# Row sums in the projection banks, another order of the projection groups, two moved products in a streaming encoder layer on eight cores

## The reference, cut to what matters

```python
q, k, v, logf, g_fox, b_gate, u, g_conv, mq, g_mem = _project(x, w_in, fox_bf)   # u = c_gate * h_in
# A) forgetting attention, 12 heads x 128, causal
s = einsum(q, k) * 128**-0.5 + cum[query] - cum[key]        # cum = cumsum(logf)
o_fox = einsum(softmax(where(causal, s, -1e30)), v)
# B) y = b_gate * conv3(u), causal, depthwise, 1536 channels; a sample's u starts with two cached columns
# C) memory cross-attention, 4 heads x 256 into 256 tokens
gates = sigmoid(x @ w_merge + b_merge)                      # g1, g2, g3
m = g1*((o_fox*silu(g_fox)) @ w_fox_out) + g2*((o_conv*silu(g_conv)) @ w_conv_out) + g3*((o_mem*silu(g_mem)) @ w_mem_out)
y = layernorm(2**0.25 * x + m @ w_o)
```

## Time and profile before

| | us |
|---|---|
| median of 3 runs | 3396.12 (3395.94 to 3399.55) |
| the profiled execution, its own time | 3396.83 |
| span of its slowest core, core 4, which the rows show | 3395.1 |
| spans of the eight cores | 3386.3 to 3395.1 |
| TensorE busy | 3283.1 |
| VectorE, ScalarE, GpSimd busy | 1227.6, 906.3, 847.0 |
| mean granted TensorE clock, core 4 | 0.991 |

### The profile page before, as it was taken

One profiled execution on the slowest core, in us unless ns is written; L12 is line 12 of the kernel. 1 busy time (PEld: TensorE's weight loads), 2 busy tenths in 40 slices (PEclk: granted clock), 3 DMA queues, 4 the chain that ended last, 5 costly groups with the idle time before them and its releaser, 6 DMA issues.

```text
span 3395.1 us, 54170 instructions; the slowest of 8 cores (3386.3 to 3395.1 us)
## 1 busy us (share of the span) xinstructions
PE 3283.1 (97%) x18645; PEld 1638.8 (48%) x18998; DVE 1227.6 (36%) x2041; ACT 906.3 (27%) x1572; POOL 847.0 (25%) x1046
## 2 busy tenths in 40 slices
PE   6999999999998999999999999999999999999998
PEld 3555555555544444444444444445544444444443
DVE  0477777777775222222211111111102331111465
ACT  0355555555553111111111111111113331111111
POOL 2233333333333222222200000222221113222233
PEclk8999999999999999999999999999999999999999
DMA  9554534343432121212134433866661115665543
GB/s 156 101 98 81 88 75 83 73 86 75 82 61 39 30 44 32 41 35 37 36 83 108 109 89 90 177 144 144 150 150 30 25 26 130 138 145 144 199 160 124
DMA packets 156405, 315.76 MB, mean 93 GB/s; under 512 B 32784, under 2 KB 60048, under 8 KB 151708
## 3 DMA queue, kind: packets, MB, share of 16 engines
q0 software_dynamic: 43840, 134.54, 24.1%
q1 hardware_dynamic: 112296, 177.73, 17.8%
HBM read 351.42 MB, written 95.32 MB: 132 GB/s over the span
## 4 chain that ended last, share of the span: by engine, by line
PE 92%; DMA 3%; issue 2%; DVE 1%; ACT 1%; POOL 0%; DVEq 0%; ACTq 0%; POOLq 0%; SPq 0%
PE bank L146 92%; DMA xT<-xTp 1%; DMA m_scr<-mt 1%; DVE st L181 0%; DMA fk_p<-k 0%; DVE acc L173 0%; ACT k L168 0%; DMA wcb<-wcM 0%; ACT rl L163 0%; DVE rr L181 0%; PE bank L149 0%; ACT sc L163 0%; ACT ge L163 0%; DVE pt L173 0%; POOL wv L155 0%
## 5 line engine op out<-in xcount | busy, mean ns | idle before, releaser
L146 PE MATMUL bank<-xT,wcb 128*128 128x512 bf16 (+1 forms) x3757 | 715.2, 342 | 9.8 <-DMA wcb<-wcM 4.7
L146 PE MATMUL bank<-xT,cwb 128*128 128x512 bf16 (+1 forms) x3766 | 693.9, 342 | 3.9 <-issue 0.2
L146 PE MATMUL bank<-xT,wkqg 128*128 128x512 bf16 (+1 forms) x2812 | 595.7, 344 | 18.3 <-DMA wkqg<-wkqg 5.9
L173 DVE TENSOR_TENSOR mt<-bank,gt 128x512 f32<-128x512 f32 (+1 forms) x240 | 143.6, 598 | 1033.8 <-PE bank L146 940.0
L146 PEld LDWEIGHTS bank<-xT,wcb 128*128 128x128 bf16 x3840 | 326.8, 98 | 366.9 <-issue 8.1
L146 PEld LDWEIGHTS bank<-xT,cwb 128*128 128x128 bf16 x3840 | 324.0, 98 | 362.4 <-issue 4.3
L163 ACT ACTIVATE pt<-st,ncc 128x512 bf16<-128x512 f32 (+4 forms) x492 | 318.7, 649 | 396.4 <-DVE st L181 306.6
L163 ACT ACTIVATE gt<-bank,bm 128x512 f32<-128x512 f32 (+1 forms) x240 | 147.1, 613 | 964.0 <-PE bank L146 959.8
L146 PEld LDWEIGHTS bank<-xT,wkqg 128*128 128x128 bf16 x2880 | 244.6, 98 | 270.7 <-issue 27.6
L181 DVE SCALAR_TENSOR_TENSOR st<-bank,cq 128x512 f32<-128x512 f32 x480 | 291.6, 608 | 172.0 <-PE bank L146 155.3
L173 DVE TENSOR_TENSOR acc<-acc,pt 128x512 f32<-128x512 f32 (+3 forms) x396 | 260.4, 658 | 0.4
(11 more groups left out here) (148 smaller groups left out, 2624.8 us busy)
## 6 DMA issues: line engine op xcount, KB each, us to landing
m_scr<-mt SPq DMA_DIRECT2D x128, 256.0 KB, 2.2
pv<-m_scr SPq DMA_DIRECT2D x128, 256.0 KB, 4.8
cwb<-wc POOLq DMA_DIRECT2D x10, 2048.0 KB, 15.1
mw<-wm POOLq DMA_DIRECT2D x16, 1024.0 KB, 12.2
x<-xp SPq DMA_DIRECT2D x16, 1024.0 KB, 7.0
y_p<-rr SPq DMA_DIRECT2D x16, 1024.0 KB, 4.8
wkqg<-wkqg POOLq DMA_DIRECT2D x40, 384.0 KB, 9.0
wcb<-wcC POOLq DMA_DIRECT2D x16, 896.0 KB, 9.0
```

The costliest lines, as they stand in the source:

```text
L146: return lambda e: e.matmul(out, lhsT=lhsT, rhs=rhs, start=start, stop=stop)
L173: return lambda e: e.tensor_tensor(out=out, in0=in0, in1=in1, op=op)
```

## The change

It does five things.

- **Banks of the row sums.** `s2` takes its bank from `nextbank` and no longer from the pair 2 and 3. An assertion records that no group is open in the bank. Nothing else of the row sum changes.
- **Order of the fill.** For heads 1 to 11 the order of the groups was k0 q0, k1 g0 q1 g1, k2, k3, k4, q4 g4, q2 g2, q3 g3 with v groups ahead of each of k1 to k4 (k1 and k2 missing for head 1). It is now k0 q0, then k1 g0 q1 k2 g1 k3 q4 g4 with the v groups spread over all of these, then q2 k4 g2 q3 g3.
- **The cached columns.** The copy of two columns into `us` is VectorE's and no longer GpSimd's, 12 times in the kernel.
- **The end of attention.** After the last tile, `s1` is run, then the first group (C, block 0) of conv block 1, then the row sum `s2` and the finish; conv block 1 goes on with its fifth piece.
- **The end of the third combine.** Of the last two items, 46 and 47, the units ran in pairs, block by block: 46/0, 47/0, 46/1, 47/1 and so on. Now they run 46/0, 46/1, 47/0, 46/2, 47/1, 46/3, 47/2, 46/4, 47/3, 47/4.

```diff
 def nextbank():
         b = (0, 1, 7)[pj[0] % 3]
         pj[0] += 1
+        assert b not in busy_banks
         return b
...
                 def s2():
                     assert pown[hi] == (i, 0) and pown[lo] == (i, 1)
-                    lb = 2 + take("s", 2)
+                    lb = nextbank()
...
-                    S.add(POOL, COPY(conv["us"][:, 0:2], sconvT[:, :, c]), reads=[r_late], writes=[r_us])
+                    S.add(DVE, COPY(conv["us"][:, 0:2], sconvT[:, :, c]), reads=[r_late], writes=[r_us])
...
-            rest = []
-            for tb in (1, 2, 3, 4):
-                if h > 0 or tb > 2:
-                    rest.append(k_group(n, tb))
-                if tb == 1:
-                    rest += [g_group(n, 0, past_block[0]), q_group(n, 1, past_block[1]), g_group(n, 1, past_block[1])]
-            nv = (len(vs) // 4 + len(rest) - 1) // len(rest)
-            for grp in rest:
-                fill += vs[:4 * nv] + grp
-                vs = vs[4 * nv:]
-            assert not vs
-            fill += q_group(n, 4) + g_group(n, 4)
-            for tb in (2, 3):
-                fill += q_group(n, tb, past_block[tb]) + g_group(n, tb, past_block[tb])
+            rest = [k_group(n, 1)] if h > 0 else []
+            rest += [g_group(n, 0, past_block[0]), q_group(n, 1, past_block[1])]
+            rest += [k_group(n, 2)] if h > 0 else []
+            rest += [g_group(n, 1, past_block[1]), k_group(n, 3), q_group(n, 4), g_group(n, 4)]
+            nv, nr = len(vs) // 4, len(rest)
+            for k, grp in enumerate(rest):
+                fill += vs[4 * (nv * k // nr):4 * (nv * (k + 1) // nr)] + grp
+            fill += q_group(n, 2, past_block[2]) + k_group(n, 4) + g_group(n, 2, past_block[2])
+            fill += q_group(n, 3, past_block[3]) + g_group(n, 3, past_block[3])
...
-    for due, fn in later:
+
+    now[0] = None
+    ps = conv_pieces(1, True)
+    later[0][1]()
+    run_all(ps[:4])
+    for due, fn in later[1:]:
         fn()
...
     for c in range(1, 12):
-        ps = conv_pieces(c, True)
-        run_all(ps[:16])
+        if c > 1:
+            ps = conv_pieces(c, True)
+        run_all(ps[4 if c == 1 else 0:16])
...
+    units = [(k, tb) for k in range(len(ITEMS) - 2) for tb in range(5)]
+    ka, kb = len(ITEMS) - 2, len(ITEMS) - 1
+    units += [(ka, 0), (ka, 1), (kb, 0), (ka, 2), (kb, 1), (ka, 3), (kb, 2), (ka, 4), (kb, 3), (kb, 4)]
```

More of the change, by code:

```diff
@@ L461, in build @@
     pj = [0]
+    busy_banks = set()
     def nextbank():
@@ L474, in fn @@
                     st["b"] = nextbank()
+                    busy_banks.add(st["b"])
                 for c in range(c0, c0 + step):
@@ L477, in fn @@
                 if c0 + step == n:
+                    busy_banks.discard(st["b"])
                     evict(st["b"])
@@ L1024, in build @@
         merge_pieces(mp, fill)
-    for due, fn in later:
+    now[0] = None
[3 more added lines that the diff above has]
+    for due, fn in later[1:]:
         fn()
     later[:] = []
-    now[0] = None
     M.free("qT0", "qT1", "qT2", "qT4", "sg0", "sg1", "sg2", "sg4", "qs0", "qs1", "sgs0", "sgs1", "cq", "cqs0", "cqs1", "kT1", "vb1", "kcT", "vc",
```

## The result

The changed kernel takes 3359.39 us, against 3396.39 for the kernel before beside it: a ratio of 0.9889, 95% interval 0.9872 to 0.9906.

What follows compares the result with a forecast made beforehand. TensorE, busy 3283.1 of 3395.1 us, was taken as the bound, so only its idle or low-clock time could be won. The terms summed to 33.6 us on core 4, giving 3363 us, range 3352 to 3377.

Steps and rivals of the forecast that it cites:

- Terms 1, 2, 4: Row sums leaving the bank pair: 12.5 us won at head boundaries, 3.0 lost to new bank neighbours, 1.0 won in head 11.
- new neighbours: Eight places where a bank is asked for again sooner, behind value copies: 0.4 us lost at each, 3.0 in all.
- VectorE remains as late: Row sum in head 11 near 995 us: its 1.75 us wait goes, but VectorE's lateness limits the gain to 1.0.
- Term 3: Order of projection groups: `ge` waits go, 2.1 us; the wait at the 64-key copy and low clock behind it, 6.2.
- Term 5: Cached columns in head 11, copied by VectorE: 2.8 us won, between 1.4 with the GpSimd port lock and 5.2 unhindered.
- Term 6: End of attention: 16 conv products fill TensorE's idle time before the row sum; 5.7 us won, bounds 4.0 and 6.0.
- Term 7: Last combine: one more unit ahead of item 47 covers its weight transfer; 6.3 us won, bounds 4.5 and 6.4.
- no wait for `wcb<-wcM`: Sign at the last combine: TensorE no longer waits for item 47's weights, a wait of 4.67 us before.
- (a): Rival: stalls come back behind VectorE at boundaries and through head 11; 22 us won, 3375 us; chance 20%.
- (b): Rival: all named waits go and no new ones come; 46.6 us won, 3350 us; chance 12%.
- (c): Rival: row sums cost projection groups more banks than scores gain, making the kernel slower, 3432 us; chance 3%.
- (d): Rival: awaited transfers at the 64 keys and last combine stay late; 12.5 us less won, 3376 us; chance 5%.

Runs made afterwards that it cites:

- e1: The changed kernel with the 48 row sums taking their bank from the pair 2 and 3 again; 3373.4 us, 0.9928 of the kernel before.
- e2: The changed kernel with the old order of the projection groups in heads 1 to 11; 3370.8 us, 0.9917 of the kernel before.
- e5: The changed kernel with the copy of the two cached columns back on GpSimd; 3362.9 us, 0.9907 of the kernel before.
- e3: The changed kernel with the old end of attention, conv block 1 only behind the finish; 3363.5 us, 0.9902 of the kernel before.
- e4: The changed kernel with the units of the last two items in pairs again; 3367.4 us, 0.9911 of the kernel before.
- e6: The changed kernel with the cached columns copied early, on ScalarE, with the sample's group C; 3359.1 us, 0.9906 of the kernel before.
- e8: The changed kernel with the next head's first q group not held back at the boundary; 3344.3 us (one execution), ratio 0.9915 to the kernel before.

## Why the prediction was right, and where its terms were off

| term | forecast | cost of undoing it, mean span |
|---|---|---|
| 1, 2 and 4: row sums, new neighbours, head 11 | 12.5 - 3.0 + 1.0 = 10.5 | 12.7 (`e1`) |
| 3: order of the groups | 8.3 | 7.7 (`e2`) |
| 5: cached columns | 2.8 | 3.6 (`e5`) |
| 6: end of attention | 5.7 | 4.7 (`e3`) |
| 7: last combine | 6.3 | 6.6 (`e4`) |
| sum | 33.6 | 35.3, of 36.9 measured for all |

The parts add up within what five differences of 1 to 2 us each can tell, so they hardly hide or help each other.

- **Terms 1, 2, 4.** The mechanism and the size at a boundary were right, VectorE late next by 0.64 us. The waits of 0.58 for `st` were nine and not eight (one stands at 918 too), so core 4 had 14.4 + 9 x 0.58 = 19.6 us of such waits; 6.4 stay, and 13.2 are won for the 12.5. Mis-sized was the clock: the forecast charged low clock to the long stalls only and none to the boundaries. Before, core 4's slice from 525 to 530, with such a boundary in it, ran at 0.66, 1.7 us lost; and over 140 to 1060 `e1` loses 3.8 us on core 4 where the changed kernel loses 1.7. The new neighbours cost less than 3.0: no value copy is waited for, only `qs`, `qT` and `sx`, 1.4 in all. In head 11 the row sum that waited 1.75 near 995 us waits no more, but two S after it do, 0.45 and 0.87 on core 4, as "VectorE remains as late" said: 0.4 is won there for the 1.0.
- **Term 3.** Right, with its spread: the wait for `k` is 0.8 to 3.4 us by core before and 2.0 to 4.3 in `e2`. Core 4 had the largest of before, so 6.2 was an upper value for the other cores.
- **Term 5.** TensorE's wait fell by 1.6 (4.17 to 2.59), next to the 1.4 of the lock and far from 3.5. On core 4 the low clock behind it stayed (0.86 and 0.80 in the two slices from 1000 to 1010, 1.7 us), but on the seven others it went: behind the 4.17 it had cost 1.7 us on three cores and 3.4 on five. That is 2.8 us in the mean against 0.2 now, and with the 1.6 of the wait 4.2 are won. So the 2.8, taken between 1.4 and 5.2, was near by luck: the wait went by the lower end, and the clock, which the lower end left out, made up for it. `e5` costs 3.6 by the mean span, a little more than the 3.3 of core 4 and less than the 4.2, within its uncertainty.
- **Term 6.** On core 4 exactly 5.7; undone in `e3`, the same stretch costs 5.2 to 5.8 by core.
- **Term 7.** The 6.3 assumed a landing 0.5 us before the need, read from one core. Other cores land up to 2.9 us later (`e4`, 4.4 to 7.3), so four of eight still wait 0.8 to 1.9. The forecast "no wait for `wcb<-wcM`" is wrong; core 4 itself won 6.3 less its 0.80 and a tail of 0.16, which makes the 5.3.
- **The total.** Core 4 won 38.6 where 33.6 was forecast: 27.4 for the 21.6 of terms 1 to 5, the same 5.7, 5.3 for 6.3. The 5.8 too few lie in the heads. The low clock gave 5.4 where 2.8 were forecast (2.6 more), and the listed waits 20.0 where the rest of the terms has 18.8 (1.2 more). Five waits fewer are 0.8 in tails of 0.16 us, which the view of waits doesn't print, and four idle times of 0.16 that it puts down to issue are gone as well, 0.6. The last 0.6 isn't placed.
- **The rivals.** (a) had VectorE right as the next limit, but the boundaries kept their gain. (b)'s 3350 needed all waits to go; 16 us stay. (c) didn't come: no projection group waits for ScalarE's `rl`. (d) holds for a part of term 7 on four cores.

What no run tells apart: the last 1.6 us between 35.3 and 36.9, and the scatter of 4 us in the slowest core, to which the waits for `mt` early in the second combine (none to 4.3 us by core and run) contribute.

## What to carry to other kernels

A wait is a pair, a resource and the work that could have stood in front of it: before giving the resource another home, look whether the schedule holds independent work back at just that place, since here one argument of one line, put into the kernel before, won 22 us where the whole change won 37. Where a transfer is waited for, take its landing on every core and cover the latest, not that of the core on the page. And where a small instruction is moved to another engine to break a wait, look at what the engine left behind is running at that moment; if both use a shared port, the price moves along.

## What the runs showed of the hardware

- The lock between VectorE and GpSimd can't be stepped around by removing its first victim: in `e6` a chain short by 1.24 us met the same two products with its next two instructions, and TensorE's wait for its end fell by 0.46.
- A copy of 128x2 elements took 1.24 us on VectorE beside a GpSimd product, 0.16 without one, and 0.19 on GpSimd itself.
- The clock's price came in pieces of about 1.7 us: core 4 before lost 1.7 at 525, 3.4 around 965 and 1.7 at 1030; over 140 to 1060 the cores 1, 3, 4 and 6 lose 5.1, 3.4, 7.1 and 5.2 before, 0, 0, 1.7 and 0 in the changed kernel, 1.7, 0, 1.7 and 1.7 in `e8`. The same stall brings it on one core and not on another: before, core 4's slice after the cached columns ran at 0.66, and in the changed kernel core 4 lost 1.7 there and the seven others nothing, behind equal waits of 2.6. What decides isn't shown by these runs.
